# A decoder layer's expert stage: sums kept in the residual rows, weight runs of 8 KB, and an earlier scatter of the ninth tile's list entries

## What is computed

```python
p_group = softmax(xn @ w_router_group + b)        # 4 groups, the best one
top_p, top_i = top_k(softmax(fine of that group), 2)   # 2 of its 8 experts
gates = g_w[:, None] * top_p / sum(top_p)
# expert e, for its tokens:  w_gate, w_up (1024 x 512), w_down (512 x 1024), float32
hb = silu(xb @ w_gate[e]) * (xb @ w_up[e])
y[tok] += gate * (hb @ w_down[e])
x = x2 + y
out = rms_norm(x, norm_final)
```

## Time and profile before

| | |
|---|---|
| median of 3 runs | 1842.24 us (1838.51 to 1843.33) |
| profiled execution, its own time | 1843.73 us |
| its span | 1842.1 us |
| mean granted clock of PE | 0.976 |
| PE / DVE / ACT / POOL busy | 1772.8 / 1151.8 / 864.0 / 469.8 us |
| DMA | 333.19 MB, mean 181 GB/s |

### The profile page before, as it was taken

How to read it: one execution, slowest core, us unless ns; L and a number is a source line. 1 busy time by engine, 2 the same in 40 slices (tenths; PEclk the granted TensorE clock), 3 DMA queues, 4 the chain that set the end, 5 groups by cost and what they waited for, 6 DMA issues and landing times. The chain is left out here.

```text
span 1842.1 us, 29038 instructions
## 1 busy us (share of the span) xinstructions
PE 1772.8 (96%) x9908; PEld 1526.1 (83%) x9908; DVE 1151.8 (63%) x1952; ACT 864.0 (47%) x1554; POOL 469.8 (26%) x496
## 2 busy tenths in 40 slices
PE   7989999999999999999989999969999999999997
PEld 6878887999999788888879978758888888888872
DVE  5267665311111354545455556779999999999985
ACT  5255555311111232333232223357877788777863
POOL 3022232000000322323231112233565333332320
PEclk9989999999999999999999999969999999999998
DMA  7121211332213203030304643279999999999987
GB/s 232 46 56 38 54 47 47 93 93 69 81 55 90 60 27 91 24 93 23 94 2 143 198 147 104 95 287 380 382 387 382 387 384 383 388 385 388 386 327 287
DMA packets 177068, 333.19 MB, mean 181 GB/s; under 512 B 36800, under 2 KB 105968, under 8 KB 175904
## 3 DMA queue, kind: packets, MB, share of 16 engines
q1 hardware_dynamic: 154912, 278.07, 41.9%
q0 software_dynamic: 21408, 53.27, 8.4%
q10 hardware_dynamic: 672, 0.85, 0.3%
HBM read 304.11 MB, written 46.35 MB: 190 GB/s over the span
## 5 line engine op out<-in xcount | busy, mean ns | idle before, releaser
L2824 POOL DMA_INDIRECT y_d<-e_y,e_idxs x32 | 138.8, 4337 | 217.5 <-DVE e_y L2928 204.0
L2899 DVE TENSOR_TENSOR e_Lg<-e_rawg,e_Hg 128x1024 fp32r<-128x1024 f32 x128 | 148.3, 1220 | 7.5 <-ACT e_Hg L2848 7.4
L2899 DVE TENSOR_TENSOR e_Lu<-e_rawu,e_Hu 128x1024 fp32r<-128x1024 f32 x128 | 147.8, 1215 | 0.0
L2899 DVE TENSOR_TENSOR e_Ld<-e_rawd,e_Hd 128x1024 fp32r<-128x1024 f32 x124 | 143.2, 1214 | 0.0
L2848 ACT ACTIVATE e_Hg<-e_rawg 128x1024 fp32r<-128x1024 f32 x128 | 125.0, 1050 | 7.2 <-DMA e_rawg<-in_w_gate 6.8
L2848 ACT ACTIVATE e_Hu<-e_rawu 128x1024 fp32r<-128x1024 f32 x124 | 120.9, 1058 | 0.0
L2848 ACT ACTIVATE e_Hd<-e_rawd 128x1024 fp32r<-128x1024 f32 x124 | 120.7, 1049 | 0.0
L162 PE MATMUL bank<-r_wH,xH 128*128 128x512 f32 x256 | 105.9, 414 | 2.4 <-DVE r_gs L1510 2.4
L162 PE MATMUL bank<-e_Hg,e_xH 128*128 128x512 f32 x256 | 102.0, 398 | 2.9 <-DVE e_xL L2905 2.9
L162 PE MATMUL bank<-e_Hu,e_xH 128*128 128x512 f32 x256 | 102.9, 402 | 0.0
L164 PE MATMUL bank<-r_wH,xL 128*128 128x512 f32 x256 | 101.6, 397 | 0.0
(11 more groups left out here) (464 smaller groups left out, 4724.2 us busy)
## 6 DMA issues: line engine op xcount, KB each, us to landing
e_rawg<-in_w_gate SPq DMA_DIRECT2D x128, 512.0 KB, 9.2
e_rawu<-in_w_up SPq DMA_DIRECT2D x128, 512.0 KB, 8.3
e_rawd<-in_w_down SPq DMA_DIRECT2D x124, 512.0 KB, 8.8
raw<-in_w_in SPq DMA_DIRECT2D x51, 512.0 KB, 4.0
c_Y<-y_d SPq DMA_DIRECT2D x8, 1024.0 KB, 13.9
m_t<-b_m_s POOLq DMA_DIRECT2D x8, 528.0 KB, 3.4
m_gate<-gate_t POOLq DMA_DIRECT2D x8, 528.0 KB, 3.9
m_m<-m_t POOLq DMA_DIRECT2D x8, 528.0 KB, 3.9
```

The lines of the kernel that those rows point to most:

```text
L2824: pool.indirect_dma_start(out=ch.y_d, out_offset=bass.IndirectOffsetOnAxis(ap=idx[:, e % IDX, 1:2], axis=0), in_=y[:], in_offset=None, bou ...
L2899: dve.tensor_tensor(L[kind][:, q], raw[kind][:, q], H[kind][:, q].bitcast(F32), ALU.subtract).then_inc(w_lo[kind], 1)
```

## The change

Four things, all after the mixer:

1. A weight load covers two chunks, 1 MB with runs of 8 KB per partition (`expert_run`); it waits for the low parts of both chunks that it overwrites. For w_down two neighbouring rows of the matrix then share a partition, so PE transposes h with a stride of two elements (`h_runs`).
2. In POOL's program the ninth tile's scatters (`fill(NT - 1)`) come ahead of the gather of expert 0. Two more tiles are cleared before them.
3. Experts are renumbered on the host so that consecutive ones come from groups 0, 1, 2, 3, 0, ... Tokens of four consecutive experts are then all different.
4. y_d is gone. The gates go to memory once (`store_gates`). For each expert POOL gathers the gates of its pairs (e_gate) and the present residual rows of its tokens (e_acc, `sums_so_far`), after the scatter of the expert four before has landed. ACT scales its half by the gate while it evacuates, and POOL adds the residual half to it; DVE does both for the other half in one instruction. The scatter writes the sums back to x2_d. `Combine` is left with a read of x2_d, the norm and the store; PE has no part in it, and x_tiles is gone. `Beyond` does the same for its blocks.

The diff, cut to its core:

```diff
-    c["groups"] = np.broadcast_to((np.arange(NE) // EPG).astype(np.float32), (P, NE)).copy()
+    c["groups"] = np.broadcast_to((np.arange(NE) % NG).astype(np.float32), (P, NE)).copy()
...
-                for q in range(NQ):
-                    expert_chunk(sp, ch, kind, 0, q)
+                for half in range(NR):
+                    expert_run(sp, ch, kind, 0, half)
...
-            pool.memset(ch.e_rows[:], 0.0).then_inc(ch.e_go, 1)
+            for t in (ch.e_rows, ch.e_acc, ch.e_gate):
+                pool.memset(t[:], 0.0).then_inc(ch.e_go, 1)
             fill(NT - 2)
+            fill(NT - 1)
             for s in range(2):
                 n = 16 * ((NT + 1 - s) // 2)
                 pool.wait_ge(x2_st[s], n)
                 pool.wait_ge(xn_st[s], n)
-            pool.wait_ge(ch.e_go, 1)
+            pool.wait_ge(ch.e_go, 3)
             expert_gather(pool, ch, 0)
-            fill(NT - 1)
             pool.wait_ge(scat, 16 * 2 * NT)
             expert_slots(pool, ch, 1)
...
-def expert_chunk(sp, ch, kind, e, q, into=None):
+def expert_run(sp, ch, kind, e, half, into=None):
 
     w = {"g": ch.w_gate, "u": ch.w_up, "d": ch.w_down}[kind][ds(e, 1)]
-    dst = ch.e_raw[into or kind][:, q]
+    dst = ch.e_raw[into or kind][:, 2 * half:2 * half + 2].rearrange("p q n -> p (q n)")
     if kind == "d":
-        src = w.rearrange("o (k p) n -> p (o k) n", p=P)[:, q, :]
+        src = w.rearrange("o (h p r) n -> p (o h) (r n)", p=P, r=2)[:, half, :]
     else:
-        src = w.rearrange("o (p k) n -> p (o k n)", p=P)[:, q * 1024:(q + 1) * 1024]
-    sp.dma_start(dst, src).then_inc(ch.e_w_in[into or kind][q], 16)
+        src = w.rearrange("o (p k) n -> p (o k n)", p=P)[:, half * 2048:(half + 1) * 2048]
+    sp.dma_start(dst, src).then_inc(ch.e_w_in[into or kind][half], 16)
...
     ORDER = (8, 0, 1, 2, 3, 4, 5, 6, 7)
-    ON_PE = {8: (0, 1), 1: (2, 3), 3: (4, 7), 5: (5, 6), 6: (0, 1)}
-    ON_DVE = (0, 2, 4, 7)
-    AHEAD = {0: 2, 2: 4, 6: 7}
...
-            sp.dma_start(self.Y[0:m, t], ch.y_d[2 * t * P:2 * (t * P + m), :].rearrange("(p k) d -> p k d", k=2)).then_inc(self.y_in[t], 16)
+            sp.dma_start(self.X[0:m, t], ch.x2_d[t * P:t * P + m, :]).then_inc(self.x_in[t], 16)
...
+            act.wait_ge(self.x_in[t], 16)
+            if n:
+                act.wait_ge(self.sq_done, n)
+            act.activation(self.junk[0:m], self.X[0:m, t], ACT.Square, accum_out=stat[0:m, t, 0:1]).then_inc(self.sq_done, 1)
...
+            dve.scalar_tensor_tensor(out=X[0:m, t], in0=X[0:m, t], scalar=stat[0:m, t, 3:4], in1=gain[0:m], op0=ALU.mult, op1=ALU.mult).then_inc(self.o_done, 1)
...
+        h_runs = h[:].rearrange("m (h p r) -> m h r p", h=NR, r=2)
...
-                    for q in range(NQ):
-                        sp.wait_ge(w_lo[kind], (e - 1) * NQ + q + 1)
-                        expert_chunk(sp, ch, kind, e, q)
+                    for half in range(NR):
+                        sp.wait_ge(w_lo[kind], (e - 1) * NQ + 2 * half + 2)
+                        expert_run(sp, ch, kind, e, half)
...
-                for t in range(NT):
-                    m = rows_of(t)
-                    sp.dma_start(ch.x2_tiles[0:m, t], ch.x2_d[t * P:t * P + m, :]).then_inc(ch.x2_in, 16)
...
+                def store_gates():
+                    pool.wait_ge(ch.gates_done, NT)
+                    pool.dma_start(ch.gates_d[0:2 * SEQ, :].rearrange("(t p k) o -> p t (k o)", t=NB, k=2), ch.gates[:, 0:NB, :]).then_inc(gates_st, 16)
+                    pool.dma_start(ch.gates_d[2 * SEQ:, :].rearrange("(p k) o -> p (k o)", k=2), ch.gates[0:NS, NB, :]).then_inc(gates_st, 16)
+                    pool.wait_ge(gates_st, 32)
+
+                def sums_so_far(e):
+                    pool.indirect_dma_start(out=gate[:], out_offset=None, in_=ch.gates_d,
+                                            in_offset=bass.IndirectOffsetOnAxis(ap=idx[:, e % IDX, 1:2], axis=0),
+                                            bounds_check=2 * T - 1, oob_is_err=False).then_inc(gate_in, 16)
+                    if e >= NG:
+                        pool.wait_ge(y_st, (e - NG + 1) * 16)
+                    pool.indirect_dma_start(out=acc[:], out_offset=None, in_=ch.x2_d,
+                                            in_offset=bass.IndirectOffsetOnAxis(ap=idx[:, e % IDX, 0:1], axis=0),
+                                            bounds_check=T - 1, oob_is_err=False).then_inc(acc_in, 16)
+
                 def scatter(e):
                     pool.wait_ge(y_a, e + 1)
+                    pool.wait_ge(acc_in, e * 16 + 16)
+                    pool.tensor_tensor(y[:, 0:512], y[:, 0:512], acc[:, 0:512], ALU.add).then_inc(y_sum, 1)
+                    pool.wait_ge(y_sum, e + 1)
                     pool.wait_ge(y_b, e + 1)
-                    pool.indirect_dma_start(out=ch.y_d, out_offset=bass.IndirectOffsetOnAxis(ap=idx[:, e % IDX, 1:2], axis=0),
-                                            in_=y[:], in_offset=None, bounds_check=2 * T - 1, oob_is_err=False).then_inc(y_st, 16)
+                    pool.indirect_dma_start(out=ch.x2_d, out_offset=bass.IndirectOffsetOnAxis(ap=idx[:, e % IDX, 0:1], axis=0),
+                                            in_=y[:], in_offset=None, bounds_check=T - 1, oob_is_err=False).then_inc(y_st, 16)
...
                     if e >= 1:
                         scatter(e - 1)
+                    else:
+                        store_gates()
+                    sums_so_far(e)
...
                 def out_evac(e):
                     act.wait_ge(used["d"], e * NQ + 2 * NQ)
                     act.wait_ge(y_st, e * 16)
-                    act.activation(y[:, 0:512], Y[0][:], ACT.Copy).then_inc(y_a, 1)
+                    act.wait_ge(gate_in, e * 16 + 16)
+                    act.activation(y[:, 0:512], Y[0][:], ACT.Copy, scale=gate[:, 0:1]).then_inc(y_a, 1)
...
                 def out_evac(e):
                     dve.wait_ge(used["d"], e * NQ + 2 * NQ)
                     dve.wait_ge(y_st, e * 16)
-                    dve.tensor_copy(y[:, 512:1024], Y[1][:]).then_inc(y_b, 1)
+                    dve.wait_ge(gate_in, e * 16 + 16)
+                    dve.wait_ge(acc_in, e * 16 + 16)
+                    dve.scalar_tensor_tensor(out=y[:, 512:1024], in0=Y[1][:], scalar=gate[:, 0:1], in1=acc[:, 512:1024],
+                                             op0=ALU.mult, op1=ALU.add).then_inc(y_b, 1)
...
-                        tr = pe.transpose(HT[:, k * P:(k + 1) * P], h[:, k * P:(k + 1) * P], ch.ident[:])
+                        tr = pe.transpose(HT[:, k * P:(k + 1) * P], h_runs[:, k // 2, k % 2], ch.ident[:])
...
-        a = np.ascontiguousarray(inputs[name])
+        a = np.asarray(inputs[name])
+        if name in expert_axis:
+            n = expert_axis[name]
+            a = a.reshape(a.shape[:n] + (NG, EPG) + a.shape[n + 1:]).swapaxes(n, n + 1).reshape(a.shape)
+        a = np.ascontiguousarray(a)
```

More of the change, by code:

```diff
@@ L2426 @@
 NQ = 4
+NR = 2
 IDX = 8
@@ L2523, in gpsimd @@
         pool.memset(idx[:], 0).then_inc(self.go, 1)
-        pool.memset(rows[:], 0.0).then_inc(self.go, 1)
-        pool.wait_ge(self.go, 2)
+        for t in (rows, self.gate, self.acc):
+            pool.memset(t[:], 0.0).then_inc(self.go, 1)
+        pool.wait_ge(self.go, 4)
         self.each(pool, body)
@@ L2620, in sync @@
             dst = ch.y_sample if t == NB else ch.y_prompt[t * P:(t + 1) * P, :]
-            sp.dma_start(dst, self.Y[0:m, t, 0]).then_inc(self.o_st, 16)
+            sp.dma_start(dst, self.X[0:m, t]).then_inc(self.o_st, 16)
         sp.wait_ge(self.o_st, 16 * NT)
-    def diagonals(self, act):
-        for i, t in enumerate(self.ON_PE):
-            m = rows_of(t)
-            for k in range(2):
-                act.activation(self.diag[0:m, i, k, 0:m], self.ch.ident[0:m, 0:m], ACT.Copy, scale=self.ch.gates[0:m, t, k:k + 1]).then_inc(self.diag_done, 1)
     def scalar(self, act):
-        stat, pe_tiles, order = self.stat, list(self.ON_PE), self.ORDER
+        stat, order = self.stat, self.ORDER
         def square(n):
@@ L2657, in scalar @@
         square(0)
-        for t in range(NT):
-            if t + 1 < NT:
-                square(t + 1)
-            root(t)
+        for n in range(NT):
+            if n + 1 < NT:
+                square(n + 1)
+            root(n)
     def vector(self, dve):
-        Y, x2, stat, gates, gain = self.Y, self.ch.x2_tiles, self.stat, self.ch.gates, self.gain
-        pe_tiles, order = list(self.ON_PE), self.ORDER
-        def weigh(t):
-            i = self.ON_DVE.index(t)
-            dve.wait_ge(self.y_in[t], 16)
-            dve.scalar_tensor_tensor(out=Y[:, t, 0], in0=Y[:, t, 0], scalar=gates[:, t, 0:1], in1=x2[:, t], op0=ALU.mult, op1=ALU.add).then_inc(self.half, 1)
-            dve.wait_ge(self.half, i + 1)
-            dve.scalar_tensor_tensor(out=Y[:, t, 1], in0=Y[:, t, 1], scalar=gates[:, t, 1:2], in1=Y[:, t, 0], op0=ALU.mult, op1=ALU.add).then_inc(self.a_done, 1)
```

(30 more changed lines are left out.)

89 lines of the change are left out of this document (33 added, 56 removed).

## The result

The changed kernel takes 1863.18 us (median of 4 runs, 1862.73 to 1865.56), the kernel before 1842.78 in the same comparison: a ratio of 1.011, 95% interval 1.0095 to 1.0124. Forecast were 1830 and a range of 1819 to 1855. Both profiled executions add up step by step.

| stretch | before | after | difference |
|---|---|---|---|
| to the first hidden high part (ACT e_hH) | 1248.68 | 1245.59 | -3.1 |
| from there to PE's end (start of ACT's last e_y) | 550.2 | 582.3 | +32.1 |
| to the first read of the tail | 5.0 | 7.6 | +2.6 |
| tail, to the end of the span | 38.2 | 25.7 | -12.5 |
| span | 1842.1 | 1861.2 | +19.1 |

The account below looks back on a forecast made before the run. The prediction took PE to set the loop's period at 17.72 us per expert, with DVE and DMA close behind. From 1843.7 us, -4 (start) +4 (loop) -12 (tail) gave 1831.7, with the median 1.5 lower 1830; range 1819 to 1855.

Parts of the forecast that it names:

- The start: Way into the expert loop: earlier scatters save PE standing and cold matmuls; -4 us, bounds 0 and -6.
- The rate of the loop: Weight loads in the loop: 8 KB runs bring 2.7% more, 385 becomes 395 GB/s, 18.0 us per expert.
- The reserve: Loop: landings from 7.6 us grow by 13.5, less 14.3 from issue to need and DVE's 3.6 lead; +3 us.
- The residual gather too late: Rival, chance 0.18: residual rows reach DVE's evacuation late in the loop; at 1 us late +26, 1854 in all.
- The add takes DVE's port: Rival, chance 0.08: POOL's add holds back DVE's splits, 0.6 us per expert; +14, 1840.
- Longer runs bring no rate: Rival, chance 0.07: 8 KB runs do not quicken the loop's loads; loop +17, 1843.
- the loop's term: Expert loop: growing DMA backlog and 1 us for disturbances cost +4 us, bounds 0 and +17.
- The strided loads: PE's transposes of h with a stride of two: nothing taken, bound 0.4 us per expert or 12 us.
- The multiply-add: DVE's half of y in the loop: 0.75 us in place of the 0.68 copy, +0.06 us.
- The tail: After the loop: 4.33 MB read instead of 8.65, last scatter 0.8 us later; -12 us, bounds -10 and -15.

Follow-up runs that it names:

- before_fill: The kernel before with only the ninth tile's scatters moved ahead of the gather of expert 0; 1842.09 us, ratio 0.9994.
- after_gates_swap: The changed kernel with gates stored in 64-byte pieces and w_gate of expert 1 loaded ahead of w_down of expert 0; 1861.46 us, ratio 1.0096.
- noadd_nogate: The changed kernel without POOL's add and with the gates gathered for expert 0 only; 1856.18 us, ratio 1.0065.
- after_dve: The changed kernel with both halves of y as fused multiply-adds on DVE and no add on POOL; 1879.64 us, ratio 1.0193.
- before_8k: The kernel before with only the 8 KB runs, their release in pairs and the strided transposes of h; 1845.92 us, ratio 1.0017.
- fill_swap_8k: The kernel before with the scatters ahead, w_gate of expert 1 ahead of w_down of expert 0, and 8 KB runs for all weights; 1840.50 us, ratio 0.9977.
- fill_swap_gu8: The kernel before with scatters ahead, w_gate of expert 1 ahead of w_down of expert 0, 8 KB runs for w_gate and w_up only; 1838.56 us, ratio 0.9974.
- after_noacc: The changed kernel with the residual gather for expert 0 only, so the sums are not formed; 1850.23 us, ratio 1.0044.

## Why the prediction was wrong, step by step

**The start (-4).** Nearly right in size, -3.1 at the first e_hH, but not by the way foretold: product g of expert 1 was to start 4 us earlier and warm, and it started 2.4 us earlier and partly at the lower clock. Both POOL times came as worked out. Not seen: w_down of expert 0 waits for gather 0 to land, so gather 0's delay moves all later loads, and w_gate of expert 1 took the place of its rows as the last to come. In before_fill the scatters alone win 1.0 us, which stays; where the loads bound the loop, what is won at the start is mostly lost again (after_gates_swap).

**The rate of the loop, the step that failed.** "385 becomes 395 GB/s, 18.0 us per expert." The gain was taken from stretches with loads alone and carried over to a mix. In the changed kernel the rate did not rise but fell, to 377 GB/s, and 7.10 MB at that rate are 18.8 us. Both terms of the 18.0 were mis-sized. The longer runs are worth 1 to 2% in the kernel before (in the changed kernel 365 against 377 GB/s at equal release), not 2.7%. The third indexed stream was priced by its bytes, 0.7 us, and costs 1.05. Per expert the loads need 18.75 us (noadd_nogate); the prediction's sum held 18.0 and its 0.2 of backlog, 18.17. Over 30 experts the difference is 17 of the missing 28 us.

**The reserve.** "7.6+13.5-14.3-3.6": landings were let grow from 7.6 us. The form was right, since the loads came late at 14.8 to 15 us (14.3 was said), but two terms were not. DVE's lead of 3.6 us did not come on top of that height; that is 3 of the missing us. And the start value was wrong: "storing the gates ... so nothing" looked only at when the gates are needed, not at what happens to the loads beside their store. They landed after 12.8 us at 1246:1260, 5 us more than the sum had, and the reserve was gone by the third expert. With the add's 3 us (below) these are the 28 us, as an estimate; by the runs with 64-byte pieces the 8-byte pieces alone answer for 3 to 6 us.

**The residual gather too late** (0.18): not in this kernel, but in after_dve. (Its price was 2 us off: -4+26-12 gives 1852, not 1854.) The rows' gather lands after 8.4 us in before_8k at 1700:1750, where it was 7.3, so 1.1 us more beside 8 KB packets (0.6 had been worked out), and after 11.6 in the changed kernel; the circle still had room for it. The Trainium skill's page "DMA: Bandwidth & Descriptors", section "Queues, rings and completion order", says that an engine drains a whole packet of one queue before it turns to another; the direction of these 1.1 us agrees. **The add takes DVE's port** (0.08): some 3 us here, beside late loads; with the gather gone, 1.1 us of DVE's time and 0.63 us of the period per expert. **Longer runs bring no rate** (0.07, 1843): they do bring some, and even this case was too kind, because it too priced the stream by bytes and started from the low landings. No rival was a DMA bound from the start, though "the DMA engines are already slightly too slow" stood in the first part. The upper end of the loop's term, +17, had to be a worse mix, not merely no gain.

**The strided loads** (0 taken, 0.4 us as bound): 0.03 us per expert, 1 us (fill_swap_8k has 17.75 us per expert, fill_swap_gu8 without the stride 17.72). **The multiply-add** (+0.06): 0.74 us, as taken.

**The tail (-12).** Right behind the first read, -12.5. But the sum's -12 held the last scatter 0.8 us later, and it is 2.6 us later, so the whole term is -9.9, just outside its bound of -10. POOL issues the gather of the last expert's residual rows only behind the scatter before and the gates' gather; they land 4.39 us later, when PE has been done for 2 us. The chain of waits:

```profile
1825.66 4.39 DMA e_accs<-x_d,e_idxs
1830.19 1.27 POOL e_y L2779
...
1832.25 3.22 DMA x_d<-e_y,e_idxs
```

## What to carry to other kernels

Before work is moved out of a tail into a loop, ask which resource the loop has left: here 8.65 MB of row reads came into a loop in which the DMA engines stood at 1.00, so that the tail moved 8.65 MB where it was 12.98; 12.5 us were won there, and the loop took 32 us more. The tail was no idle place either: the DMA share was 0.85 in it before (340 GB/s). Where a growing issue-to-landing time shows that the DMA engines are just too slow, every added byte is paid at least in full once the reserve is gone, and the reserve is filled or eaten by single transfers near the start: follow it load by load from there. A rate measured on one kind of transfer is not the rate of a mix; its bound must allow for a worse one too.

## What the runs showed of the hardware

- A store of 8 KB in 1024 pieces of 8 bytes beside 1 MB loads: the DMA engines moved 156 GB/s on average for 8 us, and 254 with pieces of 64 bytes; the two kernels were then 2.6 and 6.3 us quicker. Part of the stop is left, and its cause is open. Which engines the packets sat on was not looked at.
- PE's load of a 128x128 tile of h for its transpose takes 203 ns with a stride of two elements and 139 without. (The loads for the products, dense in both kernels, take 188.) The four of an expert add 0.03 us to the period and not 4 x 64 ns = 0.26, so most of a load lies beside matmuls. The groups by form of PE's loads at 1500:1600 in before_8k, then in the kernel before:

```profile
L2994 PEld LDWEIGHTS bank<-identity,e_hs 128*128 128x128 f32 x20 | 3.2, 203 | 0.4
```

```profile
L2992 PEld LDWEIGHTS bank<-identity,e_hs 128*128 128x128 f32 x20 | 2.5, 139 | 0.7
```

- A gather of 66 rows per expert costs 0.7 us of a full DMA system with rows of 2 KB, 1.05 with 4 KB: the first half of the bytes costs twice what the second does. If the source of the rows makes no difference (it was another one for the 2 KB rows), part of the price goes by row, not by byte.
- POOL's indexed transfers take 1 to 2 us to issue, or 4.3 to 5.3. In the loop of the kernel before the length goes with DVE: of 33 issues under 1.5 us 32 have hardly a split beside them, and the 30 long ones lie beside DVE's runs of splits for most of their time. But this is no rule: in the changed kernel 59 of 95 issues under 1.5 us lie beside splits for over nine tenths of their time, and only two are long. What sets the length is open. The Trainium skill's page "SBUF — State Buffer", section "Who interferes with whom", says that a DVE instruction with two SBUF inputs contends with a GpSimd instruction that reads SBUF; after_noacc agrees for POOL's add (DVE 5.72 us in place of 4.62).
